# Two operations of 1024 columns or one of 2048: lowering the weight tiles of a two-block transformer kernel

## The reference

```python
for l in range(DEPTH):                       # layer0, layer1
    h = x * (1.0 + sc1) + sh1
    z = h @ w_in[l] + b_in[l]                # chunks A, B, C and the gates
    m = ga * (ya @ w_pa) + gb * (yb @ w_pb) + gc * (yc @ w_pc)
    x = _layernorm(ALPHA * x + gt1 * (m @ w_out), ...)
    u, g = jnp.split(h @ w_up, 2, axis=-1)   # up
    conv = b_conv + up[:, 0:S_] * w_conv[0] + up[:, 1:1+S_] * w_conv[1] + up[:, 2:2+S_] * w_conv[2]
    y = (jax.nn.gelu(conv, approximate=False) * g) @ w_down
    x = _layernorm(ALPHA * x + gt2 * y, ...)
# middle: gated delta rule (qkv, z, w_out), SwiGLU (up, down), attention (wkv, wq, w_out), router
x = layer_norm(ALPHA_2 * x + gated_deltanet(x, ...), ...)
x = layer_norm(ALPHA_2 * x + (silu(x @ w_gate) * (x @ w_up)) @ w_down, ...)
x = layer_norm(ALPHA_2 * x + swa_sink_attention(x, ...), ...)
x = layer_norm(ALPHA_2 * x + moe_swiglu(x, ...), ...)     # experts
```

## Time and profile before

| | |
|---|---|
| median of three runs | 2811.87 us (2810.12 to 2815.71) |
| the profiled execution | 2810.85 us, its span 2809.0 us |
| mean granted TensorE clock | 0.96 of 2.4 GHz |
| busy PE, DVE, ACT, POOL | 2603.5, 2164.8, 1529.8, 24.1 us |
| L2317 (the changed line) | 496.5 us in 426 operations of the largest group |
| L1773 (the raising) | 421.6 us in 426 |

### The profile page before, as it was taken

The page is one execution under the profiler, slowest core; times in us unless marked ns, Lnnn a source line. Parts: engine busy times, 40 slices in busy tenths (PEclk is TensorE's granted clock), DMA queues, the critical chain, the costliest instruction groups (busy, mean ns, idle before and its releaser), DMA issues.

```text
span 2809.0 us, 36257 instructions
## 1 busy us (share of the span) xinstructions
PE 2603.5 (93%) x13810; PEld 2209.0 (79%) x13810; DVE 2164.8 (77%) x2724; ACT 1529.8 (54%) x1824; POOL 24.1 (1%) x46
## 2 busy tenths in 40 slices
PE   7899989998998989989989988899999999999996
PEld 6677769876777789878979876788888888888885
DVE  6877777788867777667676466798988899898886
ACT  2344434543344345455533344577777777777673
POOL 0000000000000000000000000000000000000000
PEclk9989989999999999999999998799999999999998
DMA  9833436676644455543035671698998999899894
GB/s 362 296 135 114 178 122 249 227 286 244 215 156 143 136 198 203 167 160 106 31 111 198 186 237 46 239 364 343 373 360 342 365 369 365 339 372 360 343 359 166
DMA packets 104752, 671.65 MB, mean 239 GB/s; under 512 B 11984, under 2 KB 12240, under 8 KB 27136
## 3 DMA queue, kind: packets, MB, share of 16 engines
q1 hardware_dynamic: 97584, 622.08, 59.8%
q0 software_dynamic: 6992, 47.19, 5.0%
HBM read 665.03 MB, written 4.19 MB: 238 GB/s over the span
## 4 chain that ended last, share of the span: by engine, by line
PE 64%; DVE 23%; ACT 6%; issue 4%; DMA 2%; PEld 0%; DVEq 0%; SPq 0%; ACTq 0%; PEldq 0%
PE bank L857 19%; PE bank L859 19%; PE bank L858 19%; DVE W_low L2317 8%; ACT W_high L1773 3%; PE bank L1291 2%; DVE work L2402 1%; DVE arena L2307 1%; PE bank L1644 1%; DVE work L2634 1%; DMA W<-in_w_layer 1%; DMA W<-in_w_middle 1%; DVE acted L2617 1%; DVE work L2632 1%; DVE arena_parts L2623 1%
## 5 line engine op out<-in xcount | busy, mean ns | idle before, releaser
L2317 DVE TENSOR_TENSOR W_low<-W,W_high 128x1024 fp32r<-128x1024 f32 x426 | 496.5, 1207 | 283.7 <-ACT W_high L1773 278.4
L1773 ACT ACTIVATE W_high<-W 128x1024 fp32r<-128x1024 f32 x426 | 421.6, 1039 | 398.5 <-PE bank L859 192.3
L858 PE MATMUL bank<-W_low,arena_parts 128*128 128x512 f32 (+1 forms) x1128 | 445.2, 395 | 0.0
L857 PE MATMUL bank<-W_high,arena_parts 128*128 128x512 f32 (+1 forms) x984 | 397.3, 404 | 29.0 <-DVE W_low L2317 16.1
L859 PE MATMUL bank<-W_high,arena_parts 128*128 128x512 f32 (+1 forms) x984 | 389.2, 396 | 0.0
L859 PE MATMUL bank<-hT_high,W_low 128*128 128x256 f32 (+2 forms) x1208 | 345.6, 286 | 0.0
L857 PE MATMUL bank<-hT_high,W_high 128*128 128x256 f32 (+1 forms) x1088 | 314.8, 289 | 14.8 <-DVE W_low L2317 14.8
L858 PE MATMUL bank<-hT_low,W_high 128*128 128x256 f32 (+1 forms) x1088 | 309.0, 284 | 0.0
L857 PE MATMUL bank<-W_high,hT_high 128*128 128x512 f32 (+1 forms) x640 | 264.0, 413 | 24.8 <-DVE W_low L2317 10.0
L857 PE MATMUL bank<-arena_parts 128*128 128x512 f32 x672 | 269.5, 401 | 5.3 <-DVE x L3660 3.7
L858 PE MATMUL bank<-W_low,hT_high 128*128 128x512 f32 (+1 forms) x672 | 266.8, 397 | 0.0
(11 more groups left out here) (437 smaller groups left out, 4731.6 us busy)
## 6 DMA issues: line engine op xcount, KB each, us to landing
W<-in_w_layer SPq DMA_DIRECT2D x170, 1024.0 KB, 4.9
W<-in_w_expert SPq DMA_DIRECT2D x148, 1024.0 KB, 5.1
arena<-in_w_expert SPq DMA_DIRECT2D x114, 1024.0 KB, 4.8
W<-in_w_middle SPq DMA_DIRECT2D x58, 1024.0 KB, 5.0
arena<-in_w_layer POOLq DMA_DIRECT2D x40, 1024.0 KB, 7.2
consts<-in_w_expert SPq DMA_DIRECT2D x37, 1024.0 KB, 4.8
R<-in_w_expert SPq DMA_DIRECT2D x37, 1024.0 KB, 4.8
R<-in_rows_layer SPq DMA_DIRECT2D x70, 256.0 KB, 5.9
```

Source lines behind the costliest of these rows:

```text
L857: mm(bank, lhs[0], rhs[0], start=start, stop=False)
L858: mm(bank, lhs[0], rhs[1], start=False, stop=False)
L1773: do(high_slot(at, w)[:, cols], raw(at, w)[:, cols], ACT.Copy).then_inc(main_highs.filled[main_highs.slot(at, w)], 1)
L2317: tt(lows(at, w)[:, cols], raw(at, w)[:, cols], high_slot(at, w)[:, cols].bitcast(F32), ALU.subtract).then_inc(*low_ready.event(at))
```

## The change

`lower_weight` lowers a tile in one operation over its whole width. DVE waits until both raised halves are there (`main_highs.full`). The operation gives the tile's first count of `low_ready`; then DVE waits for that count and gives the second one with an empty instruction, so that the number of counts stays as it was. Nothing else is edited: loading, raising, PE's waits, the ring of slots and the experts stay.

```diff
             def lower_weight(at, w):
                 width = W_WIDTH.get(w[0], HALF)
-                for n, cols in enumerate((slice(0, width // 2), slice(width // 2, width))):
-                    dve.wait_ge(*main_highs.part(at, w, n + 1))
-                    tt(lows(at, w)[:, cols], raw(at, w)[:, cols], high_slot(at, w)[:, cols].bitcast(F32),
-                       ALU.subtract).then_inc(*low_ready.event(at))
+                dve.wait_ge(*main_highs.full(at, w))
+                tt(lows(at, w)[:, 0:width], raw(at, w)[:, 0:width], high_slot(at, w)[:, 0:width].bitcast(F32),
+                   ALU.subtract).then_inc(*low_ready.event(at))
+                dve.wait_ge(*low_ready.last(at))
+                dve.nop().then_inc(*low_ready.event(at))
```

## The result

The changed kernel takes 2928.19 us (median of four runs, 2926.59 to 2937.9) against 2810.99 for the kernel before (2807.29 to 2815.71): 1.0423 times as long, with a 95% interval of 1.0395 to 1.0451. The forecast was 2903, with a range of 2860 to 2955.

The account below looks back on a forecast made before the run. A closed DVE-ACT round bounds the layers' up-projections, PE the middle's. To the profiled 2810.85 us it added 88.5 on the chain (63.7 + 5.0 + 9.9 + 9.9) and 4 off it: 2903, range 2860 to 2955.

Parts of the forecast that it names:

- The round of ACT and DVE: Layers' up-projections: raise, lower, taps, gate, split, Gelu, raise form a closed turn of 6.46 us without slack.
- The later start: DVE's lowering starts after the second raised half instead of the first, 0.93 us later.
- The length: A tile holds DVE for 2.43 us instead of 2.28, with 0.15 for own-result wait and empty instruction.
- The turn and the up-projections: Layers' up-projections: a turn of 7.5 us instead of 6.46, adding 51 us in the two.
- The cover in the middle's up-projection: Middle's up-projection: tiles are still ready 0.9 us before PE wants them, so steps stay at 5.78 us.
- The cover in the down-projections: Down-projections: ACT raises every 5.44 us and the tile needs 4.4, so 1.0 us is left.
- the 4 us off the chain: Some 113 tiles off the chain: 4 us for the few on which PE waits already, at most 30.
- The projections: Layers' projections before the up-projections: the forecast's count had 30.0 us added there.
- only the up-projections pay: Rival: elsewhere a later DVE meets slack, so +51 us, 2862; chance 0.13.
- faster: Rival: DVE's work is the limit, one operation saves 0.13 us a tile, 29 us, 2782; chance 0.03.
- nothing: Rival: two tiles of raised weights hide the later start everywhere, 2811; chance 0.03.
- The clock falls in the up-projections: Rival: PE standing 1.76 us every up-projection turn lowers TensorE's clock, 87 us more, 2990; chance 0.13.

Follow-up runs that it names:

- experiment 1: Kernel before, still two half-width operations, but both wait until the second raised half is there: 2894.95 us, 1.0296.
- Experiment 2: The change without the wait for its own result and the empty instruction; the one operation itself counts by two: 2907.27 us, 1.0346.
- experiment 4: Merged operation only in the two layers' up-projections, halves as in the kernel before elsewhere: 2856.48 us, 1.0156.
- experiment 6: The change with two halves kept for the tiles named down and wkv: 2904.45 us, 1.0328.
- experiment 5: Merged operation everywhere except the layers' up-projections, which keep the halves of the kernel before: 2881.32 us, 1.0246.
- experiment 11: The change plus 16 thrown-away PE matmuls ahead of the third tile in the layers' down-projections: 2930.52 us, 1.0409.
- experiment 8: The change with the lowering moved behind the taps, gate and split in DVE's loop over the hidden units: 2852.97 us, 1.015.
- experiments 9: The change plus 16 thrown-away PE matmuls ahead of the first tile in the layers' down-projections: 2927.23 us, 1.0398.

## Why the prediction was right, and what it mis-sized

The forecast of 92.5 us more (88.5 on the chain and 4 off it) came out as 117, inside the range. The round of ACT and DVE that it was built on is shown; what it left out lies outside the up-projections, 69.9 us for 41.5, about as much as the "at most 30" that its range allowed for tiles off the chain.

- *The later start* (0.93 us): right. 1 raises the turn from 6.44 to 7.38 by nothing else.
- *The length* (2.43 us for 2.28): right, 2.44. The Trainium skill (page "VectorE: DVE Perf Modes", sections "The DRAIN you can't avoid" and "Rules for kernel authors") counts a semaphore as free and the number of operations as what to cut. Experiment 2 agrees with the first half, since the next instruction comes 2.21 us after the start of an operation that itself gives a count of two; what costs 0.23 is that DVE waits for its own result and gives the count with an empty instruction. The saving of one operation per tile is 0.07 us. The forecast's 0.15 for the wait was the sum of these two, since it counted from the end of the operation.
- *The turn and the up-projections*: 7.5 us forecast, 7.55 measured; 51 us forecast, 47.9 by the table and 46.8 by experiment 4. The two layers' up-projections were the largest term and are right.
- *The cover in the middle's up-projection*: held, 0.7 us added. ACT still raises every 5.77 us there (1591.78, 1597.55, 1603.32), and PE is busy for 137.65 of 138 us.
- *The cover in the down-projections, and the 4 us off the chain*: mis-sized. "1.0 is left" was read from the steady part and stands there; the third tile and, in layer 1 and the middle, the last one have no such cover. 21.3 us measured for 5.2, and experiment 6 shows that they go with the halves. The rows for it were at hand: PE already waited 1.05 us for the last tile of layer 1 and of the middle, and the old chain goes from L2317 to PE there (from 1209.49 and 1640.64 us on). The forecast had 0.9 each for two tiles that are left after both halves. But PE had worked on the first half meanwhile, so the wait grew by 2.0. The lower clock behind the waits and, in the middle, the later load had no term at all in the sum.
- *The projections*: 43.5 us for 30.0, also mis-sized. 14.7 of it is the wait for its own result and the empty instruction, at 0.23 us the worth of 64 tiles, where the forecast had 0.15 for each of the 53 tiles that the chain passes there: 8.0. The 26.8 of the late start alone compare with the 22.0 left of its 30.0. The old chain with its new lengths is a path of the new run, as the forecast says, but it need not be the longest: the sum was a lower bound, and the 4 us for the tiles off the chain were too few. In experiment 1 the chain through layer 0's projections is another one: it runs for 7.8% of the stretch on ACT's raising and for 24.8% on the product (L857 to L859), before for 2.8 and 34.5%. The lower clock, which the forecast had in its upper end alone ("some 10"), can be only a part of the rest: layer 0's projections grew nearly as much in experiment 5 at 0.94. How much of PE's 22.1 us more of busy time lay on the path stays open.
- *The rivals*: "only the up-projections pay" is refuted by experiment 5 (69.9 us elsewhere), "faster" by 1 and 2 together, "nothing" by the result. "The clock falls in the up-projections" named the right mechanism and the wrong place: there PE stands for mostly 1.5 to 1.8 us in nearly every turn and the window shows 1.00, but behind single waits of 2.27 and 3.06 us in layer 1's down-projection it shows the lower level. The page on the clock that favoured it (the Trainium skill, "TensorE: Matmul & The Clock Gate", section "What's actually happening"), with the low level as the one that PE rests at, agrees with experiment 11, where PE was kept at work and the clock stayed at 1.00; but what that rival would have cost in the up-projections, 87 us, was not paid.

## What to carry to other kernels

In a closed round of two engines the size of the hand-over is on the path: two operations of half the width let the second engine start after the first half, and that was worth 0.93 us a turn against 0.07 for one instruction less. Before such an operation is made cheaper or coarser, look whether it must stand in the round at all: moving the lowering behind the taps and the split gave 25 us on the kernel before and 75 on the changed one. A cover read from the steady part of a loop must be read again at its first and last turn, where the order of the loops can be another. And a sum along the old chain is a lower bound on what a delay costs: an engine that comes later also changes which paths are longest, and when transfers start.

## What was not expected of the hardware

TensorE's granted clock did not follow the length of a wait alone. Waits of mostly 1.5 to 1.8 us in nearly every turn of 7.55 us left it at 1.00. Behind single waits of 2.27 and 3.06 us in the change the next seven or so matmuls came 0.43 us apart, but in experiment 8 a wait of 3.06 us at the same place left them at 0.23. A wait of 0.9 us with 1.05 us of one-column matmuls behind it was followed by the lower clock in experiments 9 and 11 and not in the change. What decided it besides the wait itself, no run here shows.
